# A gated-delta stage on one Trainium2 core: later heads' projections and half the output projection moved into the chain, four heads prepared at once

## The reference, cut to what matters

```
proj = h @ w_in
qkv = silu(causal_depthwise_conv(proj[..., :3 * GDN_DIM], conv_w))
z = proj[..., 3 * GDN_DIM:4 * GDN_DIM]
q = l2norm(q) * GDN_HEAD_DIM ** -0.5
k = l2norm(k)
o = chunk_gated_delta_rule(q, k, v, g, beta)
o = rmsnorm(o, norm_g) * silu(heads(z))
return o.reshape(bsz, seq, GDN_DIM).astype(h.dtype) @ w_out
```

## Time and profile before

| | us |
|---|---|
| Median of 3 runs (lowest, highest) | 3886.77 (3882.24, 3892.0) |
| The profiled execution, its own time | 3886.8 |
| Its span | 3885.0 |
| Mean granted TensorE clock of it | 0.958 of 2.4 GHz |
| First gated-delta stage, from its first projection to the end of its output projection | 223.6 to 516.1 |
| Second one | 1998.4 to 2295.1 |

### The profile page before, as it was taken

The page is one execution under the profiler, slowest core; times in us unless marked ns, Lnnn a source line. Parts: engine busy times, 40 slices in busy tenths (PEclk is TensorE's granted clock), DMA queues, the critical chain, the costliest instruction groups (busy, mean ns, idle before and its releaser), DMA issues. The chain is left out here.

```text
span 3885.0 us, 45081 instructions
## 1 busy us (share of the span) xinstructions
PE 3564.5 (92%) x18342; PEld 2997.1 (77%) x18342; DVE 2276.5 (59%) x2608; ACT 1839.1 (47%) x2400; POOL 606.9 (16%) x208
## 2 busy tenths in 40 slices
PE   7998799999899996899998799899998789999999
PEld 6887677788778876688887688787878568787887
DVE  4475458776566667656666454555555554555654
ACT  4453257665356562456554244444443344444443
POOL 0001129572042320142400200000000000000000
PEclk9998899999999998899998899999999899999999
DMA  5542046665276752376743035454544115354453
GB/s 217 188 148 87 1 174 239 225 240 204 101 271 233 275 206 106 134 258 238 265 166 131 1 109 189 153 189 149 198 163 164 62 68 194 142 200 157 152 195 136
DMA packets 89978, 653.57 MB, mean 168 GB/s; under 512 B 10032, under 2 KB 10032, under 8 KB 10928
## 3 DMA queue, kind: packets, MB, share of 16 engines
q1 hardware_dynamic: 78768, 573.10, 40.4%
q0 software_dynamic: 11008, 77.60, 5.6%
HBM read 649.61 MB, written 1.05 MB: 167 GB/s over the span
## 5 line engine op out<-in xcount | busy, mean ns | idle before, releaser
L1424 DVE TENSOR_TENSOR w_lo<-raw,w_hi 128x2048 fp32r<-128x2048 f32 x540 | 1421.0, 2636 | 661.0 <-ACT w_hi L1003 660.7
L1003 ACT ACTIVATE w_hi<-raw 128x2048 fp32r<-128x2048 f32 x540 | 1031.0, 1913 | 601.2 <-PE acc L518 410.2
L516 PE MATMUL wrk<-w_hi,h_hi 128*128 128x512 f32 (+1 forms) x2496 | 973.3, 390 | 61.5 <-DVE w_lo L1424 41.4
L518 PE MATMUL wrk<-w_hi,h_lo 128*128 128x512 f32 (+1 forms) x2496 | 956.2, 383 | 0.0
L517 PE MATMUL wrk<-w_lo,h_hi 128*128 128x512 f32 (+1 forms) x2496 | 955.1, 383 | 0.0
L516 PEld LDWEIGHTS wrk<-w_hi,h_hi 128*128 128x128 f32 x2496 | 473.7, 190 | 157.8 <-DVE w_lo L1424 52.3
L2082 POOL TENSOR_TENSOR arena<-arena,c 128x2048 f32<-128x2048 f32 x92 | 492.1, 5356 | 473.1 <-ACT arena L1003 447.1
L518 PEld LDWEIGHTS wrk<-w_hi,h_lo 128*128 128x128 f32 x2496 | 472.9, 189 | 93.3
L517 PEld LDWEIGHTS wrk<-w_lo,h_hi 128*128 128x128 f32 x2496 | 474.0, 190 | 85.2 <-issue 0.2
L516 PE MATMUL acc<-w_hi,hid_hi 128*128 128x512 f32 x1144 | 447.9, 392 | 9.4 <-DVE hid_lo L1507 9.4
L518 PE MATMUL acc<-w_hi,hid_lo 128*128 128x512 f32 x1144 | 445.9, 390 | 0.0
(11 more groups left out here) (254 smaller groups left out, 3501.4 us busy)
## 6 DMA issues: line engine op xcount, KB each, us to landing
raw<-in_wts SPq DMA_DIRECT2D x540, 1024.0 KB, 4.8
arena<-in_mods POOLq DMA_DIRECT2D x72, 1024.0 KB, 5.2
const<-in_const SPq DMA_DIRECT2D x1, 2176.0 KB, 10.1
c<-in_bias POOLq DMA_DIRECT2D x8, 256.0 KB, 3.4
x<-in_x SPq DMA_DIRECT2D x1, 1024.0 KB, 5.3
c<-in_c SPq DMA_DIRECT2D x1, 1024.0 KB, 4.8
out<-x SPq DMA_DIRECT2D x1, 1024.0 KB, 3.9
row<-in_rows SPq DMA_DIRECT2D x1, 512.0 KB, 11.5
```

Source lines behind the costliest of these rows:

```text
L516: nc.tensor.matmul(o, l_h, r_h, start=first, stop=False, skip_group_check=True)
L518: return nc.tensor.matmul(o, l_l, r_h, start=False, stop=last, skip_group_check=True)
L1003: return nc.scalar.activation(o, i, f, **kw)
L1424: tt(w_lo[:, ns % SLOTS, :], raw[:, ns % SLOTS, :], w_hi[:, ns % SLOTS, :].bitcast(F32), ALU.subtract).then_inc(lo_ready, 1)
```

## The change

The 16 pieces of q, k, v and z are put into another order (GDN_ORDER), so that the first six hold q, k and v of heads 0 to 3. They go to acc instead of wrk, with a semaphore of their own (side_taken). A piece is cut into two units of 24 matmuls. Twelve units stay in the first stretch; units 12 to 23 (q, k and v of heads 4 to 7) stand at four places in the first preparation, 24 to 28 between the first half's state steps, and 29 to 31 in the second preparation. The first four parts of the output projection stand between the second half's state steps. The preparation works on four heads at once, in instructions of up to 1024 columns. Splits of weights, taps, silu, and gating and splitting of the first half's output stand between the levels of the inversions on ScalarE and VectorE. z is copied first and gets its silu in the second inversion. The number of projection matmuls is the same; GpSimd's list is unchanged.

Below, the added lines of the core, in the order of the file: order and banks; TensorE; ScalarE; VectorE. In them `piece(f)` splits up to piece f, and in `invert` the function `jobs(lv)` is called behind each level.

```diff
+GDN_ORDER = [0, 1, 4, 5, 8, 9, 2, 3, 6, 7, 10, 11, 12, 13, 14, 15]
...
+    u = ["gates", "cols"]
     for half in range(2):
+        u += [f"D{half}{p}" for p in range(2)] + [f"ss{half}{p}" for p in range(4)]
+        for n in ("kk", "B", "kq"):
+            u += [f"{n}{half}{p}" for p in range(2)]
+        u += [f"tr{half}{p}" for p in range(3)]
...
+                def side(f, part):
+                    pe.wait_ge(lo_ready, ns + 1 + f + 1)
+                    if f >= BANKS and part == 0:
+                        pe.wait_ge(side_taken, a0 + f - BANKS + 1)
+                    o, s = acc[:, f % BANKS, :], (ns + 1 + f) % SLOTS
+                    for q in range(4 * part, 4 * part + 4):
+                        for b in range(2):
+                            c0 = q * 256 + b * P
+                            m = products(o[:, b * T:(b + 1) * T], w_hi[:, s, c0:c0 + P], w_lo[:, s, c0:c0 + P],
+                                         h_hi[:, q, :], h_lo[:, q, :], q == 0 and b == 0, q == KC - 1)
+                    if part == 1:
+                        m.then_inc(w_used, 1)
+                def sides(units):
+                    for u in units:
+                        side(u // 2, u % 2)
...
+                sides(range(12))
...
+                def prepare(half, first, second, third, fourth):
+                    k, heads = 2 * g + half, range(half * HALF, half * HALF + HALF)
+                    pairs = (heads[0:2], heads[2:4])
+                    for p in range(2):
+                        row_of(f"D{half}{p}", pairs[p], 0)
+                    pe.wait_ge(stage("gdn_sq"), k + 1)
+                    for p in range(4):
+                        mm(put(f"ss{half}{p}"), cst("ones"), h[:, 2 * p:2 * p + 2, :], start=True, stop=True).then_inc(filled, 1)
+                    sides(first)
+                    pe.wait_ge(stage("gdn_qk"), 2 * k + 2)
+                    for p in range(2):
+                        scores(f"kk{half}{p}", pairs[p], g_k)
+                    for p in range(2):
+                        row_of(f"B{half}{p}", pairs[p], 1)
+                    sides(second)
+                    for p in range(2):
+                        scores(f"kq{half}{p}", pairs[p], g_q)
+                    sides(third)
+                    for j, (a, s) in enumerate(((g_v, tok(0)), (g_v, tok(1)), (g_k, tok(0)))):
+                        o = put(f"tr{half}{j}")
+                        for b, n in enumerate(heads):
+                            m = tr(o[:, b * P:(b + 1) * P], a[:, n, s], cst("ident"))
                         m.then_inc(filled, 1)
+                    sides(fourth)
+                def invert(half):
...
+                def with_z(at):
+                    if at < 5:
+                        sides([24 + at])
+                def with_out(at):
+                    part = lambda *a, **kw: out_part(i, ns + 17, h0, *a, **kw)
+                    if at == 0:
+                        pe.wait_ge(side_taken, a0 + 16)
+                        part(0, 0, wait=True, qs=range(2))
+                    elif at == 1:
+                        part(0, 0, wait=True, qs=range(2, 4))
+                    elif at == 2:
+                        part(0, 1).then_inc(w_used, 1)
+                    elif at == 4:
+                        part(1, 0)
+                    elif at == 5:
+                        part(1, 1).then_inc(w_used, 1)
+                prepare(0, range(12, 16), range(16, 18), range(18, 20), range(20, 24))
+                invert(0)
+                states(0, with_z)
+                prepare(1, [29], [30], [], [31])
+                invert(1)
+                states(1, with_out)
+                out_second(i, ns + 17, h0)
...
+                def take(f):
+                    p, v = GDN_ORDER[f], acc[:, f % BANKS, :]
+                    act.wait_ge(w_used, ns + 1 + f + 1)
+                    if p >= 12:
+                        act.wait_ge(side_taken, a0 + f)
+                        fn(g_z[:, 2 * (p - 12):2 * (p - 12) + 2, :].rearrange("p a b -> p (a b)"), v, ACT.Copy).then_inc(side_taken, 1)
+                        return
...
+                for f in range(6):
+                    split_to(ns + 3 + f)
+                    take(f)
+                    if f:
+                        silu(f - 1)
+                silu(5)
...
+                def prepare(half):
+                    k, n0 = 2 * g + half, half * HALF
+                    if half == 0:
+                        act.wait_ge(h_lo_ready, before(i, "h"))
+                    steps.mark(fn(h[:, 0:4, :], g_q[:, n0:n0 + 4, :], ACT.Square))
+                    fn(h[:, 4:8, :], g_k[:, n0:n0 + 4, :], ACT.Square).then_inc(stage("gdn_sq"), 1)
+                    for p in range(2):
+                        full(f"D{half}{p}")
+                        v = bk(f"D{half}{p}").rearrange("p (a b) -> p a b", b=T)[:, :, P:T]
+                        fn(g_eg[:, 2 * p:2 * p + 2, :], v, ACT.Exp).then_inc(stage("gdn_eg"), 1)
+                    done_(f"D{half}1")
+                    fn(flat(g_ed), flat(g_ed), ACT.Exp).then_inc(stage("gdn_ed"), 1)
+                    for p in range(4):
+                        label, r = f"ss{half}{p}", (g_rq, g_rk)[p // 2]
                         full(label)
                         frees(use[name, label])
+                        fn(flat(r[:, 2 * (p % 2):2 * (p % 2) + 2, :]), bk(label), ACT.Ln, bias=EPS).then_inc(taken, 1)
+                    for p, r in ((1, g_rq), (3, g_rk)):
+                        act.wait_ge(taken, use[name, f"ss{half}{p}"] + 1)
+                        fn(flat(r), flat(r), ACT.Exp, scale=-0.5).then_inc(stage("gdn_rr"), 1)
...
+                def silu_rest(lv):
+                    if lv < 3:
+                        piece(12 + lv)
+                        if lv == 2:
+                            nc.scalar.preload_act_table_set("silu_and_others")
+                        return
+                    act.wait_ge(side_taken, a0 + 2 * lv + 2)
+                    v = dst[lv - 3][:, HALF:2 * HALF, :]
+                    fn(v, v, ACT.Silu).then_inc(stage("gdn_silu"), 1)
+                    if lv == 5:
+                        nc.scalar.preload_act_table_set("natural_log_exp_and_others")
+                def silu_gate(lv):
+                    if lv == 0:
+                        piece(18)
+                        nc.scalar.preload_act_table_set("silu_and_others")
+                    elif lv < 3:
+                        n = HALF * (lv - 1)
+                        act.wait_ge(side_taken, a0 + 16)
+                        fn(g_z[:, n:n + HALF, :], g_z[:, n:n + HALF, :], ACT.Silu).then_inc(stage("gdn_zsilu"), 1)
+                        if lv == 2:
+                            nc.scalar.preload_act_table_set("natural_log_exp_and_others")
+                    elif lv < 5:
+                        gated(2 * (lv - 3))
+                prepare(0)
+                for f in range(6, 10):
+                    piece(f + 2)
+                    take(f)
+                take(10)
+                take(11)
+                invert(0, silu_rest)
+                copy_out("u0_0", g_u0)
+                copy_out("S_0", g_s)
+                take(12)
+                piece(15)
+                copy_out("u1_0", g_vi[:, 0:4, :])
+                take(13)
+                squares(0)
+                piece(16)
+                output_norms(0, lambda q: None)
+                act.wait_ge(stage("gdn_on"), 4 * g + 2)
+                act.wait_ge(stage("gdn_silu"), 9 * g + 9)
+                prepare(1)
+                take(14)
+                piece(17)
+                take(15)
+                invert(1, silu_gate)
+                copy_out("u0_1", g_u0)
+                copy_out("S_1", g_s)
+                copy_out("u1_1", g_vi[:, 0:4, :])
+                squares(1)
+                piece(19)
+                output_norms(1, lambda q: gated(HALF + 2 * q))
...
+                def taps(f):
+                    p = GDN_ORDER[f]
+                    dve.wait_ge(stage("gdn_tap"), 12 * g + f + 1)
+                    dve.wait_ge(side_taken, a0 + f)
...
+                for f in range(6):
+                    taps(f)
+                    split_to(ns + 3 + f)
...
+                def prepare(half, jobs):
+                    k, n0 = 2 * g + half, half * HALF
+                    for p in range(2):
+                        label = f"D{half}{p}"
+                        dve.wait_ge(stage("gdn_eg"), 2 * k + p + 1)
+                        frees(label)
+                        for b in range(2):
+                            n = n0 + 2 * p + b
+                            for t in range(2):
+                                m = ts(g_ed[:, 2 * p + b, tok(t)], bk(label)[:, b * T + t * P:b * T + (t + 1) * P], decay_col(n, t), 0.0, ALU.subtract, ALU.min)
+                                if (b, t) != (1, 1):
+                                    steps.mark(m)
+                        m.then_inc(taken, 1)
+                    for r, a in ((0, g_q), (1, g_k)):
```

(73 more changed lines are left out.)

293 lines of the change are left out of this document (113 added, 180 removed).

## The result

The changed kernel took 3821.3 us in the median of four runs (3812.9 to 3823.0), the kernel before 3885.3 in its four. The ratio is 0.9829, with a 95% interval of 0.9814 to 0.9844: 64 us less. I had said 3825, between 3800 and 3858.

The account below looks back on a forecast made before the run. TensorE, busy 3564.5 of 3885.0 us, was taken as the bound, with gains only where it idles or runs at half clock. Terms summed to -30.8 us a stage, -61.6 for two: 3886.8 to 3825 us, range 3800 to 3858.

Parts of the forecast that it names:

- A: First stretch of projections: ten of 16 pieces leave it, -60.0 us a stage; its start at half clock stays.
- B: From the last early projection to the first sum of squares: 7.7 us instead of 2.8, +4.9 us a stage.
- C: First preparation with six pieces added: TensorE ends it, 49 us against 28.0, +21 us a stage.
- D: First inversion: first level at full clock, taps and splits fit between levels; -3 us a stage.
- E: First state steps and norm, with five half pieces: 28.9 us against 20.1, +8.8 us a stage.
- F: Second preparation: half pieces hidden in it, 26.7 us against 29.2, -2.5 us a stage.
- rival of a larger gain: Clock stays high throughout, second preparation and second inversion included: -38 us a stage, 3811 us; chance 0.12.
- G: Second inversion: VectorE waits for ScalarE's copies and contends with GpSimd; +1.5 us a stage.
- H: Second state steps and output projection: output products fill gaps, new waiting takes part back; -1.5 us a stage.
- rival of a smaller gain: The chain holds TensorE more often: -12 us a stage, 3863 us at its far end, middle 3845; chance 0.18.
- rival of half clock: Clock stays at half through the chain, mainly the preparations: slower, +38 us a stage, 3963 us; chance 0.03.
- the moved work does nothing: Moved projections lengthen the chain by their full 60 us: 3887 us; chance 0.05, shared with an unseen stall.

Follow-up runs that it names:

- fill_gap: Changed kernel with the first two units of the first preparation moved ahead of its wait for the squares; median 3818.9 us.
- fill_lo11: fill_gap with VectorE splitting piece 11 ahead of the transposes' scalings instead of behind them; median 3813.3 us, ratio to the kernel before 0.9810.
- warm_only: Changed kernel with 42 discarded matmuls in TensorE's wait ahead of the first half's sums of squares, no real work moved; median 3826.0 us.
- out_after: Changed kernel with the first half of the output projection put back behind the second half's state steps; median 3828.9 us.
- batch_only: Changed kernel with all 32 projection units, their splits, taps and silu in front of the chain; median 3891.3 us, ratio 1.0017 to the kernel before.
- move_e_to_f: Changed kernel with two half pieces moved from the first half's state steps into waits of the second preparation; median 3818.5 us.

## Why the prediction was right

- **A, B.** 43.9 us and 7.6 us, said as about 42 and 7.7. A ran at a clock of 0.93, so its start at half clock was longer than before (0.98 over 102.2 us), which the forecast left as it was. The piece that stays last pays for its own scaling, taps and silu in the open, and TensorE waits 5.58 us there.
- **C.** TensorE bounds it: 47.86 of 47.90 us busy, said as 49. fill_gap, fill_lo11 and warm_only show three sides of it: work put into the wait comes off, until the split of piece 11 is late, and the clock is 2.7 and 2.2 us of it, said as 2. The forecast put that split half a us from being the bound; with the gap filled it was late by 2.28 us.
- **D.** First level at full clock (1.00 for the stretch), the taps and splits between levels cost nothing: behind a wait of 0.64 us at the first level its levels follow each other with no wait. In the second stage the gain was 1.5 us, since there the kernel before had 0.95 instead of 0.90.
- **E, F.** +7.8 and -2.2, said as +8.8 and -2.5. The rival of a larger gain needed the clock to stay up in F; it was 0.88 and the wait of 3.84 us ahead of the second inversion was there, said as 3.7.
- **G.** +1.9 and +2.2, said as +1.5, and by the two causes named. The Trainium skill ("SBUF — State Buffer", Who interferes with whom) says that issue order decides who blocks; the trace agrees in both directions: the lowering that came second took 2.08 instead of 0.76, and the mask that came second to a weight split took 3.07 instead of 2.36.
- **H.** -1.0 in the first stage, said as -1.5; out_after gives 0.9 us a stage for the move itself. The -3.8 of the second stage is mostly clock in the kernel before: from the first state product of the second half to the output projection it took 15.7 us there and 12.9 in the first stage, with its outputs in records of 0.64 us instead of 0.39 (first and second stage of the kernel before):

```profile
488.16 0.39 PE L799 MATMUL wrk<-arena 128*128 128x128 f32 x2
...
2261.23 0.64 PE L799 MATMUL wrk<-arena 128*128 128x128 f32 x2
```

- The rival of a smaller gain had C at +27 and E at +13; they were +19.9 and +7.8. The rival of half clock needed more than 31 us lost a stage; C ran at 0.94. That the moved work does nothing is ruled out by batch_only against the changed kernel.

The sum (-30.4 and -31.9 us, said as -30.8) is closer than its terms, and that is luck: A gave 1.7 and 1.0 us less than said, which C and E made good by 1.1 and 1.0 in the first stage and 1.6 and 0.9 in the second, and the -3.8 of H in the second was not foreseen.

Two of the signs that the prediction named read otherwise. It said that it was wrong if an inversion got longer than before, and the second one did (38.4 instead of 36.5 us). That sign contradicts its own term G of +1.5, which is what came. And it looked for GpSimd's mask delayed at one level of that inversion: the mask beside the lowering took its 2.36 us, and the lowering was delayed. The mask that took 3.07 stands beside a split of weights.

The forecast said that batching alone gives little, which holds; the -4 us a stage that I expected of it in its own run does not. Alone it costs 1 us a stage: the second preparation took 29.8 us instead of the 26 to 27 of my walk, and the second inversion, which the walk left out, 2.7 and 3.1 us more than before.

## What to carry to other kernels

Price an in-order TensorE stretch by stretch. Where TensorE is the bound a unit of independent work costs its full length (at full clock C took 45.2 us with six pieces in warm_only and 39.6 with five in fill_lo11). Where TensorE waits it costs little or nothing: five units of 3.0 us between the state steps made them 7.8 us longer than before, and a fourth unit in the second preparation cost nothing (26.5 us with four, 27.0 with three). So look for the longest waits first. Read the waits again after each move, since the next bound may be one instruction in another engine's order (here a single split, 3.3 us a stage). And where a kernel's other stages vary by 10 us, judge an edit by the length of its own stage, and then by the stretch that it touches: an untouched stretch moved a segment by up to 2.3 us and hid an effect of 0.9.

## What I had not expected

- Four heads at once, without the projections in between, was no faster than head by head. In the first stage the first preparation took 25.3 instead of 28.0 us, but the second 29.8 instead of 29.2, the state steps 21.2 instead of 20.1, where the clock was 0.81 against 0.94, and the second inversion 39.2 instead of 36.5.
- 2.6 us won by clock in one stretch shortened the segments by 2.2 and 1.1 us only (warm_only).
- The same edit moved the segments by 6.6 us in the first and 3.9 us in the second stage (move_e_to_f), though both run the same instructions. Most of the difference is not the edit's: A and C, ahead of it, were 2.3 us shorter in the first stage than in the changed kernel.
